# Router of a decoder step: selection per token tile with top-eight instructions, affine passes off VectorE, first expert weights in small pieces

## The reference

```
x = layer_norm(ALPHA * x + mix, ln1_g, ln1_b)
gp = softmax(x @ w_rg + b_rg)                  # 4 groups
g_w, g_idx = top_k(gp, 1)
ep = softmax((x @ w_re + b_re)[group g_idx])   # 8 experts of that group
e_w, e_idx = top_k(ep, 2)
gate = g_w * e_w / sum(e_w)
expert = g_idx * 8 + e_idx                     # 2 of 32 experts for each token
y[token] = sum over both: gate * (silu(x @ w_in_gate[e]) * (x @ w_in_up[e])) @ w_out[e]
x = layer_norm(ALPHA * x + y, ln2_g, ln2_b)
```

## Time and profile before

| | us |
|---|---|
| median of 3 runs | 1563.75 (1563.1 to 1563.88) |
| the profiled execution's own time | 1562.75 |
| its span in the trace | 1560.7 |
| TensorE busy | 1473.1 (94%) |
| VectorE busy | 698.0 (45%) |
| ScalarE busy | 455.3 (29%) |
| GpSimd busy | 188.4 (12%) |
| HBM read, written | 344.82 MB, 29.31 MB |

### The profile page before, as it was taken

How to read it: one execution, slowest core, us unless ns; L and a number is a source line. 1 busy time by engine, 2 the same in 40 slices (tenths; PEclk the granted TensorE clock), 3 DMA queues, 4 the chain that set the end, 5 groups by cost and what they waited for, 6 DMA issues and landing times.

```text
span 1560.7 us, 35074 instructions
## 1 busy us (share of the span) xinstructions
PE 1473.1 (94%) x14561; PEld 1193.4 (76%) x14561; DVE 698.0 (45%) x1269; ACT 455.3 (29%) x875; POOL 188.4 (12%) x360
## 2 busy tenths in 40 slices
PE   7999999999999999999999999989978887898977
PEld 7999999999988999999988879875544443454442
DVE  5766576676789663323354335684111111111104
ACT  4533635453422462213244343211100010010102
POOL 1100000000000000000000000003333232233323
PEclk9999999999999999999999999999999999899999
DMA  5222435534458422262355472949999999999996
GB/s 207 70 92 81 132 112 163 150 116 131 125 210 305 144 82 95 81 236 81 94 189 216 148 286 85 387 187 393 420 422 422 421 420 423 410 385 421 419 423 253
DMA packets 87683, 368.28 MB, mean 236 GB/s; under 512 B 13904, under 2 KB 37664, under 8 KB 73088
## 3 DMA queue, kind: packets, MB, share of 16 engines
q1 hardware_dynamic: 81408, 357.38, 60.6%
q0 software_dynamic: 6144, 8.95, 1.6%
HBM read 344.82 MB, written 29.31 MB: 240 GB/s over the span
## 4 chain that ended last, share of the span: by engine, by line
PE 75%; DMA 17%; DVE 4%; issue 1%; ACT 1%; SPq 1%; POOL 0%; POOLq 0%; DVEq 0%; ACTq 0%
PE ps L671 37%; DMA arena<-in_w 16%; PE ps L1216 8%; PE ps L815 5%; PE ps L1235 4%; PE ps L924 3%; PE ps L1068 3%; PE ps L905 3%; PE ps L766 1%; PE ps L763 1%; PE ps L935 1%; PE ps L958 1%; PE ps L1200 1%; PE ps L1008 1%; PE ps L756 1%
## 5 line engine op out<-in xcount | busy, mean ns | idle before, releaser
L1216 PE MATMUL ps<-arena,xT 128*32 128x256 f32 x4096 | 254.3, 400 | 60.8 <-DMA arena<-in_w 60.3
L1216 PEld LDWEIGHTS ps<-arena,xT 128*32 128x32 f32 x4096 | 131.7, 114 | 158.9 <-DMA arena<-in_w 41.8
L1774 DVE TENSOR_TENSOR wl<-raw,wh 128x1024 fp32r<-128x1024 f32 x151 | 183.4, 1222 | 151.7 <-ACT wh L1307 151.1
L671 PE MATMUL ps<-xh,wh 128*128 128x272 f32 x1136 | 243.2, 295 | 1.4 <-ACT tmp L1319 0.7
L671 PE MATMUL ps<-xh,wl 128*128 128x272 f32 x1136 | 234.9, 288 | 0.0
L671 PE MATMUL ps<-xl,wh 128*128 128x272 f32 x1136 | 234.2, 288 | 0.0
L671 PEld LDWEIGHTS ps<-xh,wh 128*128 128x128 f32 x1136 | 179.0, 188 | 11.8 <-issue 9.2
L671 PEld LDWEIGHTS ps<-xl,wh 128*128 128x128 f32 x1136 | 178.5, 188 | 0.0
L671 PEld LDWEIGHTS ps<-xh,wl 128*128 128x128 f32 x1136 | 177.4, 189 | 0.0
L1307 ACT ACTIVATE wh<-raw 128x1024 fp32r<-128x1024 f32 x151 | 157.9, 1055 | 36.1 <-DMA raw<-in_slabs 19.7
L2522 DVE TENSOR_TENSOR hbuf<-sg,ps 128x128 f32<-128x128 f32 x64 | 18.4, 288 | 295.8 <-ACT sg L1626 295.6
(11 more groups left out here) (456 smaller groups left out, 2364.1 us busy)
## 6 DMA issues: line engine op xcount, KB each, us to landing
arena<-in_w SPq DMA_DIRECT2D x96, 2048.0 KB
raw<-in_slabs SPq DMA_DIRECT2D x151, 512.0 KB, 4.4
bc<-acs_dram SPq DMA_DIRECT2D x16, 512.0 KB, 5.8
hs<-in_h SPq DMA_DIRECT2D x16, 512.0 KB, 5.4
out_h_sample<-hs SPq DMA_DIRECT2D x16, 512.0 KB, 4.1
kv<-in_kT SPq DMA_DIRECT2D x8, 1024.0 KB, 5.0
...
```

The source lines that it names most:

```text
L671: r = nc.tensor.matmul(ps[:, 2 * (ub % 2) + half, 0:HT], w[:, s, col], x[:, koff + kk, half * HT:half * HT + HT], start=first and kk == 0 ...
L1216: r = nc.tensor.matmul(ps[QS * c:QS * c + QS, 2, 0:2 * FQ], xT[:, s, kk % 2, kk // 2 * QS:kk // 2 * QS + QS], arena[:, at_:at_ + 2 * FQ], ...
L1774: v.tensor_tensor(wl[:, s], raw[:, s], wh[:, s].bitcast(F32), ALU.subtract).then_inc(w_lo, 1)
```

## The change

- **Selection per tile.** `select` does the work of `first_max` for one tile, or for tiles 3 and 4 together. After the group it uses one instruction that returns the eight largest of a row (`v.max`) and one that returns their positions (`v.max_index`), and it makes the one-hots from the first two positions. It is called as soon as a tile's logits are there, so that only tile 0 is left when the last logits come. `before` is built from the other side: tile 0 now has the sum of all others.
- **Ranks.** TensorE multiplies the tiles 1 to 4 ahead, and for tile 0 only 32 columns. Ranks move to PSUM bank 1 and counts to bank 6.
- **Slots.** `fixed_slots` and `indices` work with integers and have fewer steps.
- **Affine passes.** The tiles 2, 1 and 0 leave `affine`. ScalarE scales and shifts by `1/sd` and the mean in one pass (`normed`), GpSimd multiplies by `ln1_g` and adds `ln1_b`. Tiles 3 and 4 stay on VectorE. The store of tile 0 is issued by ScalarE's queue.
- **Weights.** `fetch1(1)` and `fetch1(2)` are issued as eight transfers of 512 KB instead of two of 2 MB, and `fetch1(2)` waits for the first gather only.
- **Fillers.** `turn_over` goes from 20, 10 and 10 to 0, 5, 5 and 4.

```diff
@@ SyncE
+            def fetch1_pieces(n_):
+                for half in range(2):
+                    for piece in range(PIECES):
+                        col = half * (W1S // 2) + piece * (W1S // 2 // PIECES)
+                        at_ = w1_at[n_ % 3] + col
+                        sp_.dma_start(arena[:, at_:at_ + W1S // 2 // PIECES], A["w1"][n_][:, col:col + W1S // 2 // PIECES]
+                                      ).then_inc(w1_in[n_ % 3][half], 16)
...
-            fetch1(1)
-            store_x1(TT - 1)
-            for s in range(2):
-                sp_.wait_ge(Z[f"g_in{s}"], 16)
-            fetch1(2)
+            fetch1_pieces(1)
+            sp_.wait_ge(Z["g_in0"], 16)
+            fetch1_pieces(2)
@@ TensorE
-            turn_over(20)
-            pe.wait_ge(Z["r2_v"], 1)
...
-            nc.tensor.matmul(ps[:, 6, 0:TT * NE], stri, flat(Msel[:]), start=True, stop=False)
+            pe.wait_ge(Z["r2_v"], 1)
+            nc.tensor.matmul(ps[:, 1, NE:TT * NE], ones, flat(before[:, 1:TT]), start=True, stop=False)
+            nc.tensor.matmul(ps[:, 1, NE:TT * NE], stri, flat(Msel[:, 1:TT]), start=False, stop=True)
+            nc.tensor.matmul(ps[:, 1, 0:NE], ones, before[:, 0], start=True, stop=False)
+            turn_over(5)
             pe.wait_ge(Z["r2_v"], 2)
-            nc.tensor.matmul(ps[:, 6, 0:TT * NE], ones, flat(before[:, 0:TT]), start=False, stop=True)
-            nc.tensor.matmul(ps[:, 1, 0:NE], ones, before[:, TT], start=True, stop=True)
...
-            turn_over(10)
+            nc.tensor.matmul(ps[:, 1, 0:NE], stri, Msel[:, 0], start=False, stop=True).then_inc(Z["rank_mm"], 1)
+            pe.wait_ge(Z["r2_v"], 3)
+            nc.tensor.matmul(ps[:, 6, 0:NE], ones, before[:, TT], start=True, stop=True)
...
+            turn_over(5)
...
-            turn_over(10)
+            turn_over(4)
@@ ScalarE
+            def normed(i):
+
+                t = LN_ORDER[i]
+                act.wait_ge(Z["tr_mm"], 2 * i + 2)
+                act.wait_ge(Z["ln_r"], i + 1)
+                nc.scalar.activation(x1[:, t], x1[:, t], ACT.Identity, scale=lrs[:, t:t + 1], bias=nmr[:, t:t + 1]).then_inc(Z["f_n"], 1)
...
+            normed(4)
+            act.wait_ge(Z["ln_add"], TT)
+            act.dma_start(A["x1d"].rearrange("(t c) d -> t (c d)", c=NQ)[0:P], x1[:, 0]).then_inc(Z["x1_st"], 16)
@@ GpSimd
+            for i in range(2, TT):
+                t = LN_ORDER[i]
+                pool.wait_ge(Z["f_n"], i - 1)
+                p_.done(nc.gpsimd.tensor_tensor(x1[:, t], x1[:, t], ln1_row[0][:], ALU.mult))
+                p_.sync()
+                nc.gpsimd.tensor_tensor(x1[:, t], x1[:, t], ln1_row[1][:], ALU.add).then_inc(Z["ln_add"], 1)
@@ VectorE
+                step(lambda t: v.tensor_reduce(col(gm, t), groups(t), AX.X, ALU.max))
+                step(lambda t: v.scalar_tensor_tensor(gkey[:, t], groups(t), col(gm, t), cst[:, C_G:C_G + NG], ALU.is_equal, ALU.mult))
+                step(lambda t: v.tensor_reduce(col(gkm, t), gkey[:, t], AX.X, ALU.max))
+                step(lambda t: v.tensor_scalar(gkey[:, t], gkey[:, t], col(gkm, t), 1.0, ALU.is_equal, ALU.subtract))
...
+                step(lambda t: v.max(top[:, t], mle[:, t]))
+                step(lambda t: v.max_index(at_top[:, t], top[:, t], mle[:, t]))
+                step(lambda t: v.tensor_scalar(o12[:, 0, t], iota, at_top[:, t, 0:1], None, ALU.is_equal))
+
+            def chosen(t):
+                return v.scalar_tensor_tensor(Msel[:, t], iota, at_top[:, t, 1:2], o12[:, 0, t], ALU.is_equal, ALU.add)
...
+                do(v.tensor_scalar(pairi[:, a:b], tab, float(NQ // 2), float(NQ // 2 * SKIP), ALU.mult, ALU.add))
+                v.tensor_scalar(gidx[:, a:b], pairi[:, a:b], -NQ, quad[:, 0:1], ALU.bitwise_and, ALU.bitwise_or).then_inc(Z["gi_v"], 1)
...
+                c_.done(row_of(0))
+                do(v.tensor_tensor(blkeq_f[:], wide(pairs(blki[:]), NBF), over_b(blks_f[:], NBF), ALU.is_equal))
```

More of the change, by code:

```diff
@@ L266, in build @@
         lg = small_tile("lg", [P, TT, NG + NE])
[L267 to L268 removed]
+        gm, gs, gkm, m2 = (small_tile(n_, [P, TT]) for n_ in ("gm", "gs", "gkm", "m2"))
+        gkey, gex = (small_tile(n_, [P, TT, NG]) for n_ in ("gkey", "gex"))
+        top, at_top = small_tile("top", [P, TT, 8]), small_tile("at_top", [P, TT, 8], U32)
         mle, key, Msel = (small_tile(n_, [P, TT, NE]) for n_ in ("mle", "key", "Msel"))
@@ L2353, in _ @@
             logits_of(0)
-            affine(2)
             logits_of(1)
-            logits_of(2)
-            affine(3)
-            c_.done(v.memset(before[:, 0], 0.0))
+            dve.wait_ge(Z["o_bank"], 2 * TT)
+            select(3, 4)
+            c_.done(v.memset(before[:, 3], 0.0))
+            c_.done(chosen(3))
+            do(chosen(4))
+            do(v.tensor_scalar(Msel[:, 4], Msel[:, 4], cst[:, C_VAL:C_VAL + 1], None, ALU.mult))
+            c_.done(v.tensor_copy(before[:, 4], Msel[:, 3]))
+            c_.done(v.tensor_tensor(before[:, 2], Msel[:, 3], Msel[:, 4], ALU.add))
+            second(3)
+            second(4)
+            logits_of(2)
+            dve.wait_ge(Z["o_bank"], 2 * TT + 1)
+            select(2)
+            do(chosen(2))
+            c_.done(v.tensor_tensor(before[:, 1], before[:, 2], Msel[:, 2], ALU.add))
+            second(2)
             for r_ in run:
@@ L2364, in _ @@
             c_.done(v.tensor_scalar(blks_f[:], riota[:, 0, 0:NBF], -float(NBF), None, ALU.add))
+            c_.done(v.tensor_copy(quad[:], cst[:, C_QUAD:C_QUAD + 1]))
             logits_of(3)
+            dve.wait_ge(Z["o_bank"], 2 * TT + 2)
+            select(1)
+            do(chosen(1))
+            do(v.tensor_tensor(before[:, 0], before[:, 1], Msel[:, 1], ALU.add))
+            dve.sem_inc(Z["r2_v"], 1)
+            second(1)
             norm_tile(TT - 1)
@@ L2368, in _ @@
             dve.wait_ge(Z["o_bank"], 2 * TT + 4)
[L2369 to L2390 removed]
+            select(0)
+            chosen(0).then_inc(Z["r2_v"], 1)
+            second(0)
+            dve.wait_ge(Z["r2_v"], 2)
+            v.tensor_tensor(before[:, TT], before[:, 0], Msel[:, 0], ALU.add).then_inc(Z["r2_v"], 1)
+            v.tensor_tensor(gex[:], lg[:, :, 0:NG], bc3(gm[:], NG), ALU.subtract).then_inc(Z["r1_v"], 1)
+            v.tensor_tensor(m2[:], top[:, :, 1], top[:, :, 0], ALU.subtract).then_inc(Z["r1_v"], 1)
             dve.wait_ge(Z["rank_mm"], 1)
             row = lambda ap, d_: ap[:, NE // 2 - d_:NE // 2 + NE - d_]
[L2394 to L2395 removed]
+            cnt, pre = ps[:, 6, 0:NE], cst[:, C_PRE:C_PRE + NE]
+            rank = ps[:, 1, 0:TT * NE].rearrange("p (t e) -> p t e", t=TT)
             over_t = lambda ap: ap.unsqueeze(1).to_broadcast([P, TT, NE])
```

82 lines of the change are left out of this document (35 added, 47 removed).

## The result

The changed kernel is slower: 1571.26 us in the median of five runs (1570.83 to 1573.54) against 1563.18 for the kernel before (1561.24 to 1563.88), a ratio of 1.0056 (95% interval 1.0044 to 1.0068), which is 8.8 us; the two medians differ by 8.1. I had forecast 1558.0, and given "slower" 9 in 100.

The account below looks back on a forecast made before the run. The stream of expert weights was taken as the bound, so the router's worth was starting it earlier: 1.2 - 6.9 - 0.4 + 0.5 - 2.7 + 2.6 = -5.7 us, giving 1558.0 as the median, range 1553.5 to 1563.0.

Parts of the forecast that it names:

- Selections in the middle: VectorE's list before tile 0's residual: added selections take 9.8 to 9.9 against 8.7 us of room, residual 1.2 later.
- Rival B: In each selection the two new instructions cost 1.5 us together instead of 0.6: 1562.6, no visible change; chance 11%.
- Last logits to slots: From the last logits to the first slots: only one selection and small steps remain, 3.0 for 9.9 us, so -6.9.
- Slots and rows: Slots, table and row numbers: fewer dependent steps, -0.8, table products at a lower clock, +0.4; sum -0.4 us.
- Store of tile 0: Before the first gather: tile 0's store lands almost together with the row numbers; 0.5 us added.
- Gather to turn: From first gather to its rows' turn on TensorE: with four fillers the landing decides, -2.7 us.
- The clock: First `gate_up`: TensorE starts it at 1.2 GHz after little work, so it takes 2.6 us more.
- The frame: After the router: only where the second `gate_up` ends matters, -5.7 us; later waits keep their distance from it.
- My claim that all later waits move along: Behind the router: the distance from `fetch1(3)` to the end stays 496 us.
- Rival C: Router stage: GpSimd's six passes stretch to 4.72 us each beside VectorE, delaying the store and gather: 1568.5; chance 9%.

Follow-up runs that it names:

- e1: The changed kernel without GpSimd's six passes (tiles 2, 1 and 0 get no gain or bias): 1560.1 us, ratio 0.9981.
- e6: The changed kernel without GpSimd's six passes and with more filler matmuls where TensorE idles: 1556.23 us, ratio 0.9957.
- e2: The changed kernel with the affine passes back on VectorE and tile 0's store on SyncE's queue: 1566.12 us, ratio 1.0021.
- e5: The changed kernel with each GpSimd pass over 1024 columns cut into eight over 128: 1568.02 us, ratio 1.0028.
- e7: The changed kernel without GpSimd's six passes, weights of experts 1 and 2 fetched in whole transfers instead of pieces: 1559.01 us, ratio 0.9978.
- e3: The kernel before with only the affine part of the change: 1567.85 us, ratio 1.0030.
- e10: The kernel before with 4 last fillers instead of 10: 1563.25 us, ratio 0.9999.
- e4: The kernel before with a gauge at its end: fourteen small VectorE instructions, each issued during a GpSimd pass; the pass took 2.34 us in all fourteen.

## Why the prediction was wrong

The forecast's terms beside what the profiled executions gave, in us against the kernel before, from the table above. e1 and e6 leave out GpSimd's passes; e6 has more fillers than the change, so its last two terms aren't the change's.

| | forecast | changed | e1 | e6 |
|---|---|---|---|---|
| residual of tile 0 | +1.2 | +9.4 | +1.3 | +1.3 |
| residual to last logits | 0 | +1.3 | +1.0 | 0.0 |
| last logits to slots | -6.9 | -2.3 | -6.4 | -6.8 |
| slots to gather | -0.4 + 0.5 | +0.5 | -0.3 | +0.7 |
| gather to `gate_up` | -2.7 | -2.0 | -2.1 | -2.3 |
| length of the first `gate_up` | +2.6 | +2.4 | +1.7 | -0.1 |
| second `gate_up` ends | -5.7 | +9.4 | -4.6 | -7.0 |
| behind it | 0 | -0.9 | +2.5 | +0.5 |

1. *Selections in the middle, +1.2: this step failed.* I counted VectorE's room as if its instructions ran at their own speed beside GpSimd's four passes for tiles 2 and 1. The residual came 9.4 later. Without the passes it came 1.29 later, so instruction counts and prices were right: the index pair took 0.53 from start to start (`MAX8` 0.20, then 0.09 and 0.18) where I took 0.6. Rival B falls. The other 8.1 are the holds.

2. *Last logits to slots, -6.9.* Right without the passes, by e1 and e6. In the changed kernel it was 7.9 instead of 10.2, the same failure: tile 0's two passes, and the memsets behind them, made two instructions 4.6 longer. I also left out that the last logits themselves come 1.05 to 1.3 late when the clock has fallen in the gap ahead of them, as in e1, e2, e5 and the changed kernel; in e7 it had not, with the same gap as in e1.

3. *Slots and rows, -0.4:* e1 -0.3, the changed kernel +0.5.

4. *Store of tile 0, +0.5:* it didn't limit in the changed kernel, since the holds had put it off until 16 us after `fetch1(1)` was issued; it landed in 2.6. That is luck. Where it was issued 5.4 to 6.3 us after that fetch, with the weights still under way, it landed 8.1 (e1, e7), 8.3 (e6) and 9.7 (e3) after its issue, 13.5 to 16.0 after the fetch's. My 2.6, with 4.0 at most, was too low for that. I also left `fetch1(1)` at its place, while it waits behind the store of tile 1 and so for GpSimd: 29.96 after the first residual addition in the changed kernel, 29.99 in e3, 27.34 before. Had nothing been held, the store would have landed at 43.5 to 46.0 (29.96 plus 13.5 to 16.0) against row numbers at 39.8 by the forecast. This is an estimate from these rows that no run tests; by it this term is +3.6 to +6.1, and half or more of the forecast gain was gone even without holds.

5. *Gather to turn, -2.7:* -2.0 in the changed kernel, -2.2 in e1, -2.1 in e10. Right in kind, within the bounds.

6. *The clock, +2.6:* the group took 2.45 more in the changed kernel. Right there, though it is 1.2 to 1.8 in e2, e10, e7, e1 and e5.

The frame held for the comparison that was forecast: the rest behind the second `gate_up` is 495.2 where it was 496.1. It isn't a constant, though: it is 1.3, 2.5 and 3.4 longer in e2, e1 and e5, each in a single execution. From `fetch1(3)` to the end it is 495.9 before, 495.0 in the changed kernel and 498.4 in e1. My claim that all later waits move along is thus too strong for differences of a few us. With the passes left out, the sum said -5.7 and e1 gave -3.0 by the ratio, about half.

*Rival C named the right place and got the direction wrong.* Its sign, passes of 3.9 us or more, didn't appear. I expected two engines that share an interface to slow each other, watched GpSimd's passes, and asked how far they could stretch before tile 0 was late. They don't stretch; VectorE stops. That C's 1568.5 lies near the 1571.26 measured is luck. The Trainium skill's sentence that I used ("GPSIMD Engine Reference", section Specifications: contention with VectorE instructions in a two-port mode or with two SBUF inputs) agrees with e4's two-operand forms row for row. e4's one-operand forms from SBUF were held too; whether they ran in a two-port mode no row shows. That sentence doesn't say who waits; the trace does. I should have priced it from VectorE's side: six passes of 2.36 = 14 us in which most of the selection can't run. Two fifths of that cancel the forecast gain of 5.7.

The cause of the loss is thus shown. Up to the first slots the changed kernel is 12.4 us behind e1. The holds in its rows are 8.1 and 4.6; of these 0.6 ran beside a wait for the ranks, and the last logits add 0.25. By the ratios of e1 and the changed kernel GpSimd's passes cost 11.7 us, against 3.0 that the rest gained with those passes left out. With all of the work kept and the affine passes on VectorE (e2), the rest doesn't gain but loses 3.3.
